# Four array quarters for the gram and state products of a chunked scan, and block-diagonal operands for its level products

## The reference

```python
def rwkv7_scan(r, decay, k, v, a_vec, b_vec, s0, reverse):
    def step(S, inp):
        r_t, w_t, k_t, v_t, a_t, b_t = inp
        sa = jnp.einsum('bhij,bhj->bhi', S, a_t)
        S = S * w_t[:, :, None, :] + sa[..., None] * b_t[:, :, None, :] + v_t[..., None] * k_t[:, :, None, :]
        return S, jnp.einsum('bhij,bhj->bhi', S, r_t)
    xs = tuple(jnp.moveaxis(t, 1, 0) for t in (r, decay, k, v, a_vec, b_vec))
    S, ys = lax.scan(step, s0, xs, reverse=reverse)
    return jnp.moveaxis(ys, 0, 1), S
```

## Time and profile before

| | us |
|---|---|
| median of 3 runs (3829.46 to 3870.79) | 3829.64 |
| the profiled execution | 3845.05 |
| its span | 3843.3 |
| TensorE matmul busy, 27450 records | 3489.2 (91%) |
| TensorE weight load busy | 2955.5 (77%) |
| VectorE busy | 1812.8 (47%) |
| ScalarE busy | 1183.0 (31%) |
| GpSimd busy | 402.8 (10%) |

### The profile page before, as it was taken

One profiled execution on the slowest core, in us unless ns is written; L12 is line 12 of the kernel. 1 busy time (PEld: TensorE's weight loads), 2 busy tenths in 40 slices (PEclk: granted clock), 3 DMA queues, 4 the chain that ended last, 5 costly groups with the idle time before them and its releaser, 6 DMA issues. The chain is left out here.

```text
span 3843.3 us, 62413 instructions
## 1 busy us (share of the span) xinstructions
PE 3489.2 (91%) x27450; PEld 2955.5 (77%) x27450; DVE 1812.8 (47%) x2463; ACT 1183.0 (31%) x1648; POOL 402.8 (10%) x272
## 2 busy tenths in 40 slices
PE   5699998999999868989799998999776999999999
PEld 3487876899999747976599996777544788888887
DVE  5463545444444353226355553466342463636463
ACT  1444433221211132235544442353353211111111
POOL 0122221000000011221000002221011100000000
PEclk8799999666665579999899999999788999999999
DMA  8122233221211142132411102212111111111112
GB/s 332 47 95 88 81 121 113 68 68 36 68 35 41 52 153 99 45 127 80 170 49 61 55 19 110 86 52 80 61 44 66 50 47 50 45 51 48 51 48 73
DMA packets 145996, 294.54 MB, mean 77 GB/s; under 512 B 10048, under 2 KB 86976, under 8 KB 140224
## 3 DMA queue, kind: packets, MB, share of 16 engines
q1 hardware_dynamic: 126608, 212.95, 16.3%
q0 software_dynamic: 19120, 77.60, 6.0%
HBM read 211.22 MB, written 79.30 MB: 76 GB/s over the span
## 5 line engine op out<-in xcount | busy, mean ns | idle before, releaser
L60 PE MATMUL ev_ps<-h_hi,ev_w_hi 128*128 128x512 f32 (+1 forms) x792 | 289.0, 365 | 40.2 <-POOL ev_w_lo L360 38.9
L60 PE MATMUL ff_ps<-h_hi,ff_w_hi 128*128 128x512 f32 x768 | 300.1, 391 | 2.0 <-DVE ff_w_lo L3039 2.0
L61 PE MATMUL ff_ps<-h_lo,ff_w_hi 128*128 128x512 f32 x768 | 299.9, 390 | 0.0
L62 PE MATMUL ff_ps<-h_hi,ff_w_lo 128*128 128x512 f32 x768 | 299.7, 390 | 0.0
L61 PE MATMUL ev_ps<-h_lo,ev_w_hi 128*128 128x512 f32 (+1 forms) x792 | 281.4, 355 | 0.0
L62 PE MATMUL ev_ps<-h_hi,ev_w_lo 128*128 128x512 f32 (+1 forms) x792 | 281.3, 355 | 0.0
L3039 DVE TENSOR_TENSOR ff_w_lo<-ff_w,ff_w_hi 128x1024 fp32r<-128x1024 f32 (+1 forms) x80 | 89.5, 1119 | 339.6 <-ACT ff_w_hi L3014 339.6
L60 PEld LDWEIGHTS ev_ps<-h_hi,ev_w_hi 128*128 128x128 f32 x792 | 150.7, 190 | 79.9 <-POOL ev_w_lo L360 41.0
L3014 ACT ACTIVATE ff_w_hi<-ff_w 128x1024 fp32r<-128x1024 f32 (+1 forms) x80 | 78.0, 975 | 326.4 <-PE ff_ps L62 324.2
L60 PEld LDWEIGHTS ff_ps<-h_hi,ff_w_hi 128*128 128x128 f32 x768 | 144.9, 189 | 33.6 <-DVE ff_w_lo L3039 3.6
L62 PEld LDWEIGHTS ff_ps<-h_hi,ff_w_lo 128*128 128x128 f32 x768 | 144.9, 189 | 30.2
(11 more groups left out here) (501 smaller groups left out, 8605.5 us busy)
## 6 DMA issues: line engine op xcount, KB each, us to landing
ff_w<-in_w_up SPq DMA_DIRECT2D x48, 512.0 KB, 3.5
ev_w<-in_ev_w_in POOLq DMA_DIRECT2D x33, 512.0 KB, 3.9
ada_wt<-in_ada_w POOLq DMA_DIRECT2D x12, 1024.0 KB, 8.2
ada_wt<-in_ada_w SPq DMA_DIRECT2D x12, 1024.0 KB, 8.6
ff_w<-in_w_down SPq DMA_DIRECT2D x32, 384.0 KB, 3.0
ar<-ev_ar SPq DMA_DIRECT2D x8, 1280.0 KB, 5.4
bk<-ev_bk SPq DMA_DIRECT2D x8, 1280.0 KB, 8.0
sc_ar<-ar SPq DMA_DIRECT2D x20, 512.0 KB, 6.1
```

The costliest lines, as they stand in the source:

```text
L60: nc.tensor.matmul(out, w_hi, x_hi, start=start, stop=False)
L61: nc.tensor.matmul(out, w_hi, x_lo, start=False, stop=False)
L62: return nc.tensor.matmul(out, w_lo, x_hi, start=False, stop=stop)
```

## The change

Two things are changed in `phase_scan`. In the loops of gram, state_w, state_u and state_ys, the index that picks the quarter runs innermost: gram's h is taken into the function, and d is moved inside p and h (or j) in the state products. The waits of both directions or both halves then stand ahead of the first product, and the semaphores are released behind the last products of either direction. The level products take all 128 partitions: mD and Pm grow to 128x128 per head, block-diagonal over the two chunks with zeros outside, so that one matmul does what two did; their masks grow with them (`quarter`, `lmq`), built once at the scan's start on VectorE.

```diff
-        mD, Pm = sb("mD", [P, 2, 8, CH]), sb("Pm", [P, 2, 8, CH])
+        mD, Pm = sb("mD", [P, 2, 8, P]), sb("Pm", [P, 2, 8, P])
...
-                def gram(n, x, h):
+                def gram(n, x):
                     for d in range(2):
-                        out = (bA, bB)[h][d]
                         if x == 0:
-                            if h == 0:
-                                pe.wait_ge(ld[d, n % 2], 48 * (n // 2 + 1))
+                            pe.wait_ge(ld[d, n % 2], 48 * (n // 2 + 1))
                             if n:
-                                done(pe, ("Pev", "zf")[h], d, n - 1)
+                                done(pe, "Pev", d, n - 1)
+                                done(pe, "zf", d, n - 1)
                         else:
-                            done(pe, "mB", d, n, h)
+                            done(pe, "mB", d, n)
                         settle()
                         for p in range(4):
                             for q in range(2):
-                                r, c = half(h), half(q)
-                                last = mm(out[c, 128 * p:128 * p + 128], bk[r, n % 2, d, p, x, c], ar[r, n % 3, d, p, :, c], start=True, stop=True)
-                        last.then_inc(S[("gB", "gK")[x], d], 1)
+                                for h in range(2):
+                                    r, c = half(h), half(q)
+                                    last = mm((bA, bB)[h][d][c, 128 * p:128 * p + 128], bk[r, n % 2, d, p, x, c], ar[r, n % 3, d, p, :, c],
+                                              start=True, stop=True)
+                        last.then_inc(S[("gB", "gK")[x], d], 2)
...
                         for j in range(8):
-                            for q in range(2):
-                                c = half(q)
-                                last = mm(bA[d][c, 32 * j:32 * j + 32], mD[c, d, j], X[c, d, j], start=True, stop=True)
+                            last = mm(bA[d][:, 32 * j:32 * j + 32], mD[:, d, j], X[:, d, j], start=True, stop=True)
...
                         for j in range(8):
-                            for q in range(2):
-                                c = half(q)
-                                last = mm(bB[d][c, 32 * j:32 * j + 32], Pm[c, d, j], Z[c, d, j], start=True, stop=True)
+                            last = mm(bB[d][:, 32 * j:32 * j + 32], Pm[:, d, j], Z[:, d, j], start=True, stop=True)
...
                 def state_u(n, e):
                     for d in range(2):
-                        c = half(ORDER[d][e])
                         done(pe, "Wev", d, n, 2 * e + 1)
                         if e == 0:
                             done(pe, "zf", d, n)
-                        settle()
-                        for j in range(8):
-                            o = slice(64 * j, 64 * j + 64)
+                    settle()
+                    for j in range(8):
+                        for d in range(2):
+                            o, c = slice(64 * j, 64 * j + 64), half(ORDER[d][e])
                             last = mm(bC[d][c, o], Zf[c, n % 2, d, j], W[c, d, o], start=True, stop=True)
-                        last.then_inc(S["U", d], 1)
+                            if j == 7:
+                                last.then_inc(S["U", d], 1)
...
-                        nc.gpsimd.tensor_tensor(mD[:, d], mB[:, n % 2, d, :, 0], hm[:].unsqueeze(1).broadcast_to([P, 8, CH]),
-                                                ALU.mult).then_inc(S["blocks", d], 1)
+                        nc.gpsimd.tensor_tensor(mD[:, d].rearrange("s j (q c) -> s j q c", q=2),
+                                                mB[:, n % 2, d, :, 0].unsqueeze(2).broadcast_to([P, 8, 2, CH]),
+                                                quarter[:].unsqueeze(1).broadcast_to([P, 8, 2, CH]), ALU.mult).then_inc(S["blocks", d], 1)
...
-                        tt(Pm[:, d].rearrange("s j (a c) -> s j a c", a=2),
-                           bA[d][:, 0:256].rearrange("s (j c) -> s j c", j=8).unsqueeze(2).broadcast_to([P, 8, 2, 32]),
-                           lmh[:, d, l].rearrange("s (a c) -> s a c", a=2).unsqueeze(1).broadcast_to([P, 8, 2, 32]),
+                        tt(Pm[:, d].rearrange("s j (a c) -> s j a c", a=4),
+                           bA[d][:, 0:256].rearrange("s (j c) -> s j c", j=8).unsqueeze(2).broadcast_to([P, 8, 4, 32]),
+                           lmq[:, d, l].rearrange("s (a c) -> s a c", a=4).unsqueeze(1).broadcast_to([P, 8, 4, 32]),
                            ALU.mult).then_inc(S["Pm", d], 1)
```

More of the change, by code:

```diff
@@ L677, in phase_scan @@
     levels_ready = g.sem("sc_level_masks")
+    quarters = g.sem("sc_quarters")
     consts, zeroed = g.sem("sc_consts"), g.sem("sc_zeroed")
@@ L846, in state_w @@
                 def state_w(n, e):
-                    for d in range(2):
-                        c = half(ORDER[d][e])
-                        if n or e:
-                            m, f = (n, 0) if e else (n - 1, 1)
+                    if n or e:
+                        m, f = (n, 0) if e else (n - 1, 1)
+                        for d in range(2):
                             done(pe, "snew", d, m, f)
@@ L853, in state_w @@
                             done(pe, "y", d, m, f)
-                        else:
-                            pe.wait_ge(zeroed, 1)
-                        settle()
-                        for p in range(4):
-                            for h in range(2):
-                                o = 256 * h + 64 * p
+                    else:
+                        pe.wait_ge(zeroed, 1)
+                    settle()
+                    for p in range(4):
+                        for h in range(2):
+                            for d in range(2):
+                                o, c = 256 * h + 64 * p, half(ORDER[d][e])
                                 last = mm((bC, bD)[h][d][c, o:o + 64], ar[half(h), n % 3, d, p, 0, c], St[half(h), d, p], start=True, stop=True)
-                        last.then_inc(S["W", d], 1)
+                                if p == 3 and h == 1:
+                                    last.then_inc(S["W", d], 1)
                 def state_u(n, e):
                     for d in range(2):
-                        c = half(ORDER[d][e])
                         done(pe, "Wev", d, n, 2 * e + 1)
@@ L888, in state_ys @@
                                     mm(bD[d][r, at:at + 64], lhs, rhs, start=x % 2 == 0, stop=x % 2 == 1)
-                        for p in range(4):
-                            for h in range(2):
-                                r = half(h)
+                    for p in range(4):
+                        for h in range(2):
+                            for d in range(2):
+                                c, r = half(ORDER[d][e]), half(h)
                                 last = mm(bC[d][r, 64 * p:64 * p + 64], St[r, d, p], ar[r, n % 3, d, p, 1, c], start=True, stop=True)
-                        last.then_inc(S["YS", d], 1)
+                                if p == 3 and h == 1:
+                                    last.then_inc(S["YS", d], 1)
                 pe.wait_ge(consts, 96)
@@ L937, in _ @@
             def _(pool):
-                pool.wait_ge(consts, 96)
+                pool.wait_ge(quarters, 3)
                 for n in range(NB):
@@ L1027, in _ @@
                 dve.wait_ge(consts, 96)
+                nc.vector.memset(quarter[:], 0.0).then_inc(quarters, 1)
+                dve.wait_ge(quarters, 1)
+                for q in range(2):
+                    nc.vector.tensor_copy(quarter[half(q), q], hm[half(q)]).then_inc(quarters, 1)
+                dve.wait_ge(quarters, 3)
                 for d in range(2):
-                    tt(lmh[:, d].rearrange("s l (a c) -> s l a c", a=2), lm[:, d].unsqueeze(2).broadcast_to([P, NL, 2, 32]),
-                       hm[:].rearrange("s (a c) -> s a c", a=2).unsqueeze(1).broadcast_to([P, NL, 2, 32]), ALU.mult).then_inc(levels_ready, 1)
+                    tt(lmq[:, d].rearrange("s l (a c) -> s l a c", a=4), lm[:, d].unsqueeze(2).broadcast_to([P, NL, 4, 32]),
+                       quarter[:].rearrange("s q (a c) -> s (q a) c", a=2).unsqueeze(1).broadcast_to([P, NL, 4, 32]), ALU.mult).then_inc(levels_ready, 1)
                 dve.wait_ge(levels_ready, 2)
```

24 lines of the change are left out of this document (12 added, 12 removed).

## The result

The changed kernel takes 3955.66 us (median of 4 runs, 3952.47 to 3968.57) against 3834.68 for the kernel before (median of 4 on the same chip, 3829.46 to 3870.79): a ratio of 1.03, with a 95% interval of 1.0243 to 1.0358. It is slower, outside the forecast range, and on the side to which the prediction gave 0.05. The profiled spans differ by 111.8 us (3955.1 and 3843.3). These are the page's first lines for the changed kernel: busy us, share of the span and instructions of each engine, and the granted clock in 40 slices.

What follows compares the result with a forecast made beforehand. TensorE's pace was taken as the bound, VectorE next where the clock is high. Terms -48 + 16 - 15 - 5 + 3 + 2 = -47 us took the profiled 3845.1 to 3798, median 3783 us; range 3705 to 3845.

Steps and rivals of the forecast that it cites:

- I take 125, twice 62.6: Whole-array level products: forecast ns per record at the low clock, making a product of both directions 4.0 us.
- 107 (twice a quarter's) and 160: Level products: forecast bounds in ns for one record at the low clock; 160 is 107 and 53 in turn.
- a level product of both directions takes over 4.5 us: Level products: one of the signs named beforehand that would show the prediction wrong.
- The 62.6 ns row: First phase: 24 records loading 128 columns and streaming 2 in 1.64 us, high clock; nearest row for pricing level products.
- alternating quarters go at one record per load of 64 columns: Small products before the change: claimed pace whatever is streamed, about 55 ns low clock, 29 ns high.
- The prediction's 96 ns for state_u: state_u before the change: pace read per record for products staying in one quarter, 31 in 3.18 us.
- load and stream in turn: Level products, rival, chance 0.13: no overlap, 160 ns low and 80 high per record, total 3848 us.
- The clock up within 7 us of each block's start, in all blocks: Front of each block: expected sign, as both row halves stream all the time; front saves 3.2 us.
- and again during the second state_ys: Second state_ys: high clock expected after some 5 us, 6.9 us for 8.6, saving 1.7 a block.
- I leave the clock falling where it falls today: Middle of a block: clock's fall kept in place though TensorE's stand before p1 grows from 0.65 to 1.3 us.
- Blocks of 57 to 59 us, all alike: Steady blocks of the scan: expected length, where before six took 61 to 63 us and three 67 to 69.
- the rival of 0.22 chance: Scan blocks, chance 0.22: clock stays high through the levels, 85 us gained, about 3700 us, blocks near 48.

Runs made afterwards that it cites:

- rows_as_matmul: Kernel before, with the first phase's 24 transposes (128 weight columns, 2 streamed) written as plain matmuls with the same operands; 3842.94 us in one run.
- quarters_only: Kernel before with only the new loops of gram, state_w, state_u and state_ys; mD, Pm and level products as they were; 3693.05 us, ratio 0.9579.
- half_columns: Changed kernel with each level product issued as two of 128 rows and 64 weight columns, doubled masks kept; 3691.31 us, ratio 0.9572 to the kernel before.
- quarters_stream64: quarters_only with each level product streaming 64 columns in place of 32, its operand read twice; 3667.99 us, ratio 0.9521 to the kernel before.

## Why the prediction was wrong

**The step that failed** is the price of one record of a level product, "I take 125, twice 62.6" at the low clock and half of it at the high one, between "107 (twice a quarter's) and 160". It measured 213 and 112 ns, beyond both bounds. The same block by its steps, from 888.6 us on:

| stretch | forecast, us | measured, us |
|---|---|---|
| front, first gram to mask_v | 16.7 | 15.6 |
| mask_v and the first level product | 3.9 | 6.2 |
| middle, to the second state_ys | 17.0 | 30.5 |
| second state_ys | 6.9 | 4.2 |
| end | 13.4 | 19.8 |
| sum | 57.9 | 76.3 |

The sum is 18.4 us over the forecast, 166 us if it is taken nine times; the profiled execution is 159 us above its forecast (3956.8 and 3798). The level products alone are 24.6 us over (48.6 for 24.0); everything else together came out 6.2 us better than forecast. Had four of the eight run at each clock, as forecast, they would have taken 43.2 us (3.8 and 7.0 each). So 19.2 of the 24.6 us are the price of the record, and 5.4 are that more of them ran at the low clock. The prediction's own sign of being wrong, "a level product of both directions takes over 4.5 us", came true with 7.0.

**Why the bounds failed.** Two readings were wrong. The 62.6 ns row was of transposes; rows_as_matmul shows that matmuls with these operands take 112 at the same clock. And "alternating quarters go at one record per load of 64 columns", read as one load after another over the whole array, was the wrong mechanism: the quarters hold their tiles at the same time. The matmul paces of quarters, column halves and the whole array fit one rule, worked out from these traces: an fp32 matmul record holds its tile for about two cycles of the granted clock per weight column or per streamed column, whichever are more, and tiles that share no part of the array are held side by side. (At the low clock it fits within some 2 ns; at the high clock records take about 5 ns longer, 112 for 107 and 58 for 53, and 32x32 records fall well short of it, 9 ns for 6.7.) A level product in its quarter has 64 weight columns, 107 ns at 1.2 GHz, two quarters in turn 53 (55 read from the earlier trace rows). The prediction's 96 ns for state_u mixes two things: inside one direction's quarter the starts in the trace (939.7 to 942.7 us) lie 107 ns apart, and only where the second direction's quarter takes over are they closer. A gram has 128 streamed, 213 (0.21 in the earlier trace rows), and in four quarters 53 (the timeline above). A product over all columns has 128 weight columns, 213, and no neighbour beside it. So the merge halved the number of records and made each four times as long. Gram's row could not tell the two readings apart, since four loads at 53 ns and one stream of 213 come to the same. The second state_ys does: 160 records of 64 columns took 8.6 us at the low clock, one after another in two quarters; over four quarters they took 4.2, more than half of it at the low clock:

```profile
941.18 0.44 PE L889 MATMUL sc_bD<-sc_V,sc_Bt 64*64 64x64 f32 x8
941.39 0.44 PE L889 MATMUL sc_bD<-sc_mB,sc_U 64*64 64x64 f32 x8
...
943.63 0.29 PE L889 MATMUL sc_bD<-sc_V,sc_Bt 64*64 64x64 f32 x8
943.75 0.29 PE L889 MATMUL sc_bD<-sc_mB,sc_U 64*64 64x64 f32 x8
```

Eight records pass every 0.21 us at the low clock, 27 ns each, and every 0.12 us at the high one, 15 ns each, for 27 and 13 by the rule. One load at a time would have taken 4.3 us even at the high clock throughout.

The rival "load and stream in turn" was the right side for the wrong reason: it forecast 160 and 80 ns and 3848 us. Its load of 107 was too short, and streaming does hide behind it, since 64 streamed columns take no longer than 32 (3.79 and 3.76 us).

**The clock.** "The clock up within 7 us of each block's start, in all blocks" held, with 2.4 to 5.4 us; "and again during the second state_ys" held too, 4.2 us for 6.9. "I leave the clock falling where it falls today" was near in place: it fell at 909.3 us, in the first level product rather than in the third. But a stand of TensorE before it, which the forecast let grow with VectorE's longer mask, played no part: TensorE had not stood since 902.6 us, and did not behind the fall (30.90 us busy of 30.90). "Blocks of 57 to 59 us, all alike" failed in both parts: they take 73.5 to 78.0 us, mostly by how long the clock is high from the second state_ys on. In quarters_only, where nothing but the level products and their masks differs, the mean clock of the steady blocks was 0.77 to 0.96, against 0.63 to 0.66, and streaming twice as many columns raised it to 0.89 to 0.97 in the changed kernel. What the low clock cost are the 169 us above. Why the clock takes these products differently is open: the runs show that it does. With the old level products the rival of 0.22 chance would have been the case in some blocks, and its 3700 us is close to the 3693 measured.

**Terms that held.** state_u 1.97 us for 1.7; gram x = 0 3.7 us for 3.4 (64 records, low clock); VectorE's mask 1225 ns for 1.24 us; mD 2.37 us for 2.5. half_columns equals quarters_only in time, so neither costs anything that the total shows, though TensorE waits 13 us more for VectorE in it.

**The rules weighed against the change.** The Trainium skill, "TensorEngine Tiling (Array Packing)", Key Properties, says that changing the tiling mode drains the engine. The trace shows a small price at such places, of the size of the prediction's 0.15 us: state_u's 32 records in quarters, between whole-array products, start 0.12 us later than the pace before them gives, and the next product starts 1.90 us behind their start, where their own pace gives 1.71 (32 times 53 ns). Such changes are no cause of the loss. The same section says that different tiles load and multiply in parallel. That is the rule the change gave up in the level products, the trace agrees with it (29 ns a record in half_columns against 112), and it should have been the rule weighed against the change. The Trainium skill, "TensorE: Matmul & The Clock Gate", LDWEIGHTS, has the load at columns / 1.2 GHz, 107 ns for 128 columns. The trace disagrees at the low clock, with 213 ns for these fp32 matmuls; at the high clock its 112 is near the 107. The prediction set that figure aside for the transposes' 62.6 ns; taking it for the four products forecast at the high clock would have removed 5.6 of the 24.6 us of error (four times 1.4).

## What to carry to other kernels

In these traces the cost of a small fp32 matmul is read from the longer of its weight columns and its streamed columns, and from how many tiles of the array are held at once: put the alternation between quarters innermost, and don't merge two products on different columns into a block-diagonal one, since halves of the columns work side by side and the whole array works alone (half_columns gives the merged rows for nothing). Take the pace of an operation from rows of the same operation, not from a transpose that loads as many columns. Where the load is longer than the stream, try streaming more columns: here it cost nothing and kept the clock high (quarters_stream64, 4.8% faster than the kernel before), while going below quarters to 32x32 tiles lost more to stands of TensorE than the faster records gave, the supply of instructions being the likely cause.

## What the runs showed of the hardware

- Doubling the streamed columns of the level products made three kernels faster, by 59 to 194 us, and a fourth by 25 us, which is not clear of the noise, at the same time per product.
- With TensorE recorded busy without a gap for 30.9 us, its granted clock stayed at 1.2 GHz throughout: recorded busy does not mean at the high clock.
- An fp32 matmul that loads 128 columns leaves two records, 112 ns apart at the high clock and 213 ns at the low one; a transpose with the same operands leaves one, 62.6 ns from the next.
- With 32x32 tiles records follow one another at 9 ns, but not for long: after 126 of them TensorE stood 1.77 us for "issue".
